# Setup on x and constants alone, state-space taps four to a bank, and two norms from one set of sums

## The chip, the cores and the metric

The kernel runs on one core of a Trainium2 chip, in one launch. The metric is the device time of the whole program in microseconds (us), lower is better. The engines: PE is TensorE (products and transposes; PEld are its weight loads), DVE is VectorE, ACT is ScalarE, POOL is GpSimd, and SP only issues DMAs. Each engine works through its own instructions in order and waits on semaphores for the others.

## What is computed

x has 512 positions of 1024 features (S = 512, D = 1024). Two blocks of layers follow one another:

```python
def first_block(x):
    for i in range(4):
        h = rms_norm(x, mix_norm_g[i])
        x = x + mixer(h)
        x = x + swiglu(rms_norm(x, ffn_norm_g[i]), ffn_w_gate_up[i], ffn_w_down[i])
    return rms_norm(x, final_norm_g)

def second_block(x):
    for l in range(2):
        h = rmsnorm(x, norm1_w[l]) * (1.0 + sc1) + sh1
        x = x + g1 * hybrid_mixer(h)
        h = rmsnorm(x, norm2_w[l]) * (1.0 + sc2) + sh2
        x = x + g2 * swiglu_2(h)
```

The mixers of the first block are fox attention, the S5 layer, a pooling and fox attention again; `hybrid_mixer` is a latent attention beside a state space layer. `rms_norm(x, g)` is x / sqrt(mean(x^2) + 1e-6) * g over the features. sc, sh and g1, g2 come from a small vector c and w_ada. The S5 layer is a linear state space of 64 groups with 16 channels and 64 complex states each. It is computed in chunks of eight positions: inside a chunk by a table of "taps" (the response of the layer at each distance, for the 16 x 16 channels of a group, with the skip gain d on the diagonal), between chunks by a scan of the states.

## The kernel before, in words

x lies transposed in the on-chip memory as `m.x`: 128 partitions by 8 blocks `k` of features by 512 positions. The program is a list of stages that `plan` sets up and `build` emits, each group of stages as one block: every engine has its own list of instructions, and all meet at the end of a block (the rows name L2900 or L2991 there). The two halves of a feed-forward net are one block; setup, FoxV, the S5 mixer, its GLU, the final norm and the second block's input projection are one block each. SP loads weights for the next chunks into two raw slots; a slot is free when DVE has made its low half.

Large products run as three single-pass products: weights and activations are split into a high part (ACT copies, `split_hi`, L1214) and a low part (DVE subtracts, `split_lo`, L1221). `Split.ahead(j)` prepares chunk j+1 while PE works on chunk j.

**Sums of squares.** `add_square` (L276 to L279) squares a block of x on DVE and adds it to `m.acc`. Whoever writes x calls it, `SplitDown` (L1573) in its second half for every block. `Stats` turns `acc` into 1/rms for every partition: PE sums the partitions against `mean_w` (L388), ACT takes the root (L402, after a `warm` activation at L400 that brings in the table), DVE inverts (L409) and builds four diagonal matrices (L411), PE spreads them to all partitions in bank 6 (L394). `keep_warm` (L284) issues filler matmuls. `SplitNorm` then makes h: DVE multiplies (L1185), ACT rounds to `h_hi` (L1172), DVE takes `h_lo` (L1180).

**Setup.** SP issues the constants, a table `spread` (64 x 1408 floats), x (2 MB), 18 rows of parameters, and four small loads for fox attention. PE (L2106) waits for x, for all 25 other loads and for the fills, then transposes x by blocks into four banks (L2114), and the parameters (L2117). DVE waits for the 25 loads, casts three constants, and per block copies it (L2136) and calls `add_square`; the columns come last (L2140). ACT makes `cact` and copies `spread` (L2123, L2124).

**FoxV** is the next block: ACT rounds the gate weights (L1638), DVE takes their rest (L1663), then `Stats`, then the first weight split between the diagonals and the use of bank 6, then h and the products (L1623 on).

**S5Mix.** POOL makes `v0` (eight groups q of powers of lambda times C, L941 to L947). DVE makes block-diagonal B matrices (`block(q)`, L966) in two buffers, input weights (`weights(q)`, L975 to L980), the rotation tables `ec` and `es` (`turns`, `table(n)`, L997 to L1017), and moves finished taps out (`keep(q)`, L989 and L990). PE does the input projection in four chunks f of weights (L812); `taps(q)` (L789), eight pairs of 32-row products into bank 4; `turn_w(q)` transposes the weights (L798). Behind each chunk stand taps: (0, 1), (2, 3), (4), (5, 6), then `turn_w(f)` for f < 3. `taps(q)` waits for `keep(q-1)`, since all use the same 128 columns of bank 4. Then come eight groups of transposed inputs (L824), gathered half by ACT and half by DVE (L927), `taps(7)`, and the loop of `inputs` (L838), `outputs` (L850, L852), `turn_w(q+3)` and `turn_y` (L860), in which DVE scans (L1057 to L1079). The taps go through DRAM: SP stores each q with its padding of zeros (L759), waits, and reads it back shifted in eight loads (L767), q = 0 to 2 at once, the others when a buffer is free. DVE's order is written out by hand from L1019: `block` 0 and 1, `weights(0)`, `keep(0)`, `block(2)`, `keep(1)`, `block(3)`, `weights(1)`, `turns()`, `table` 1, 2, 4 and 8, `keep(2)`, `block(4)`, `keep(3)`, `block(5)`, `weights(2)`, `table(16)`, `keep(4)`, `block(6)`, `table(32)`, `keep(5)`, `block(7)`, `keep(6)`, the eight gathers, `keep(7)`, the scans.

**FinalNorm** (L2841) is a block of its own: `Stats`, then DVE writes the normed x in place (L442) and squares it again for the next norm, then makes the gains (1 + scale) * w of the second block (L2859). **SecondIn** splits `wdt` (L2347, L2389), runs `Stats` and `SplitNorm` with those gains, and multiplies; its products (L1259 to L1261, L2333) go to banks 0 to 4, and at chunk 2 it squares latents in banks 5 and 6. x itself is not needed again before the block's output projection adds to it.

## Time and profile before

| | us |
|---|---|
| median of 3 runs | 4105.17 |
| the runs | 4106.72, 4099.12, 4105.17 |
| the profiled execution | 4099.89 |
| its span, from first to last instruction | 4098.1 |

| engine | busy us | share of the span |
|---|---|---|
| PE | 3765.1 | 92% |
| DVE | 2086.4 | 51% |
| ACT | 1073.3 | 26% |
| POOL | 1070.4 | 26% |

The mean granted clock of PE is 0.952 of full speed. Times in rows are us from the start of the span. A row of a timeline is one instruction or several alike that follow each other; "idle before" is how long the engine stood before it, and the arrow names what ended that. Rows of PE can overlap, since matmuls are pipelined.

### The profile page before, as it was taken

What the parts mean: (1) busy time and instruction counts of PE and PEld (TensorE: products, weight loads), DVE (VectorE), ACT (ScalarE), POOL (GpSimd) and SP (SyncE); (2) the same over time, 40 slices, a digit from 0 to 9 for tenths busy, and PEclk for the clock granted to TensorE, in tenths of its full rate; (3) what the DMA queues carried; (4) which work ended last, traced back from release to release, by engine and by line L of the source; (5) the groups of instructions that cost most, each with busy time, mean ns of one, the idle gap of its engine ahead of it and who ended that gap; (6) DMA issues with size and microseconds to landing.
All of it is one profiled execution on the core that took longest, in us unless ns stands there. A gap on an engine that the chain in (4) does not pass through costs nothing. (4 is left out here: it accounts for less than half of the span.)

```text
span 4098.1 us, 44475 instructions
## 1 busy us (share of the span) xinstructions
PE 3765.1 (92%) x16846; PEld 2898.0 (71%) x16846; DVE 2086.4 (51%) x2654; ACT 1073.3 (26%) x1473; POOL 1070.4 (26%) x835
## 2 busy tenths in 40 slices
PE   6889999778999979999898999897899999879999
PEld 5656888556788858887666888673578877347887
DVE  4445555775554575454445545565443345545334
ACT  2442222013221212222443222232321223332221
POOL 0342634610263416350342635001300000130000
PEclk9999999878999989999999999997899999889999
DMA  3114444211444324443112544210123322003332
GB/s 102 44 31 109 126 129 116 68 44 43 112 127 134 113 71 139 123 126 90 50 33 67 142 121 124 66 54 21 31 82 97 99 77 65 21 23 87 90 103 77
DMA packets 553376, 346.08 MB, mean 84 GB/s; under 512 B 32327, under 2 KB 534477, under 8 KB 553229
## 3 DMA queue, kind: packets, MB, share of 16 engines
q1 hardware_dynamic: 539404, 293.79, 25.5%
q0 software_dynamic: 13824, 50.34, 4.2%
q8 instruction: 91, 1.49, 0.2%
q14 instruction: 57, 0.46, 0.0%
HBM read 341.01 MB, written 3.08 MB: 84 GB/s over the span
## 5 line engine op out<-in xcount | busy, mean ns | idle before, releaser
L1259 PE MATMUL ps<-h_hi,w_hi 128*128 128x512 f32 x2880 | 1141.7, 396 | 33.0 <-DVE h_lo L2031 10.1
L1260 PE MATMUL ps<-h_lo,w_hi 128*128 128x512 f32 x2880 | 1126.1, 391 | 0.0
L1261 PE MATMUL ps<-h_hi,w_lo 128*128 128x512 f32 x2880 | 1125.7, 391 | 0.0
L1221 DVE TENSOR_TENSOR w_lo<-w,w_hi 128x2048 fp32r<-128x2048 f32 (+2 forms) x294 | 663.7, 2258 | 168.8 <-ACT w_hi L1214 166.3
L1214 ACT ACTIVATE w_hi<-w 128x2048 fp32r<-128x2048 f32 (+2 forms) x294 | 507.2, 1726 | 701.8 <-PE ps L1261 635.7
L1259 PEld LDWEIGHTS ps<-h_hi,w_hi 128*128 128x128 f32 x2880 | 544.2, 189 | 151.7 <-issue 35.4
L1261 PEld LDWEIGHTS ps<-h_hi,w_lo 128*128 128x128 f32 x2880 | 543.3, 189 | 115.2
L1260 PEld LDWEIGHTS ps<-h_lo,w_hi 128*128 128x128 f32 x2880 | 544.0, 189 | 108.4 <-issue 0.5
L1350 DVE TENSOR_TENSOR sg<-sg,ps 128x512 f32<-128x512 f32 x132 | 90.8, 688 | 719.4 <-ACT sg L1335 719.4
L1259 PE MATMUL ps<-a_hi,w_hi 128*128 128x512 f32 x1056 | 412.1, 390 | 0.0
L1261 PE MATMUL ps<-a_hi,w_lo 128*128 128x512 f32 x1056 | 411.0, 389 | 0.0
L1260 PE MATMUL ps<-a_lo,w_hi 128*128 128x512 f32 x1056 | 410.8, 389 | 0.0
L1335 ACT ACTIVATE sg<-ps 128x512 f32<-128x512 f32 x132 | 79.0, 598 | 1088.6 <-PE ps L1261 1088.5
L1132 POOL TENSOR_TENSOR w<-w,cact 128x1024 f32<-128x1024 f32 x96 | 184.5, 1922 | 452.3 <-PE ps L1318 452.0
L1134 POOL TENSOR_TENSOR w<-w 128x512 f32<-128x512 f32 x192 | 241.6, 1258 | 15.1
L1261 PEld LDWEIGHTS ps<-a_hi,w_lo 128*128 128x128 f32 x1056 | 198.2, 188 | 41.4
L1259 PEld LDWEIGHTS ps<-a_hi,w_hi 128*128 128x128 f32 x1056 | 198.2, 188 | 41.1 <-DVE w_lo L1221 0.3
L1260 PEld LDWEIGHTS ps<-a_lo,w_hi 128*128 128x128 f32 x1056 | 198.2, 188 | 41.0
L1123 POOL DMA_DIRECT2D w<-in_w_ada x96 | 88.7, 923 | 484.5 <-POOLq L2900 416.8
L1135 POOL TENSOR_TENSOR w<-w 128x128 f32<-128x128 f32 x96 | 195.1, 2032 | 7.5
L1879 POOL TENSOR_SCALAR misc<-misc,small 128x128 f32<-128x128 f32 (+3 forms) x128 | 138.1, 1086 | 204.2 <-DVE small L1896 203.9
L1911 DVE TENSOR_REDUCE small<-ps 128x1 f32<-128x128 f32 x192 | 93.2, 486 | 185.5 <-PE ps L1747 120.9
(445 smaller groups left out, 4137.9 us busy)
## 6 DMA issues: line engine op xcount, KB each, us to landing
w<-in_ffn_w_gate_up SPq DMA_DIRECT2D x176, 512.0 KB
w<-in_w_ada POOLq DMA_DIRECT2D x96, 512.0 KB, 6.9
w<-in_ffn_w_down SPq DMA_DIRECT2D x64, 704.0 KB
w<-in_w_gate_up SPq DMA_DIRECT2D x88, 512.0 KB
w<-in_w_down SPq DMA_DIRECT2D x32, 704.0 KB
w<-in_fox_w_in SPq DMA_DIRECT2D x32, 512.0 KB
w<-in_w_in SPq DMA_DIRECT2D x14, 1024.0 KB
w<-in_fox_w_in SPq DMA_DIRECT2D x8, 1024.0 KB
```

What stands on the lines that cost most here:

```text
L1123: nc.gpsimd.dma_start(three(m.ada_w[:, u % 2, :]), self.source(u)).then_inc(m.sem["ada_in"], 16)
L1132: m.pool(e, tt(three(p), three(m.ada_w[:, u % 2, :]), c, ALU.mult))
L1134: m.pool(e, tt(p[:, 0:n], p[:, 0:n], p[:, n:2 * n], ALU.add))
L1135: tt(p[:, 0:P], p[:, 0:P], p[:, P:2 * P], ALU.add).then_inc(m.sem["ada_summed"], 1)
L1214: last = nc.scalar.activation(hi, raw, ACT.Copy)
L1221: last = nc.vector.tensor_tensor(lo, raw, hi.bitcast(F32), ALU.subtract)
L1259: nc.tensor.matmul(out, hi, a[0][:, k, :], start=k == 0, stop=False)
L1260: nc.tensor.matmul(out, hi, a[1][:, k, :], start=False, stop=False)
L1261: return nc.tensor.matmul(out, lo, a[0][:, k, :], start=False, stop=k == kt - 1)
L1350: m.dve(e, nc.vector.tensor_tensor(t, m.sg[:, par(j), 0, :], m.ps[:, par(j) * 2 + 1, :], ALU.mult))
L1879: nc.gpsimd.tensor_scalar(self.pb[s % 2][t], self.pb[s % 2][t], self.stat(self.ri, s, t), None, ALU.mult).then_inc(m.sem["p_scaled"], 1)
L1911: nc.vector.tensor_reduce(self.stat(self.nm, s, t), m.ps[:, 2 + t % 2, 0:(t + 1) * P], AX.X, ALU.max, negate=True).then_inc(m.sem["max_rea ...
```

## The change

**Setup.** The constants have a semaphore of their own, and PE's transposes of x wait for them and for x alone; the parameters' transposes wait for the other 23 loads behind them. DVE only copies x. The sums of squares of the first norm are made by ACT from x as it was loaded (positions on partitions, four squares of 128 x 1024 with an accumulated output) and end as the root in `m.rms`; the first `Stats` is `known` and begins with the reciprocal. `spread` is loaded by the GLU's `sync`, as its last small load, and copied by ACT behind the GLU's third sigmoid. DVE squares the final gains into `final2`.

**S5.** `taps(0)` to `taps(3)` write four parts of bank 4, `taps(4)` to `taps(7)` four parts of bank 7; there are three `block` buffers, and two `keep`s. The zeros of the padding are stored once for all q.

**Final norm.** The stage is gone. The last down projection also sums squares of x times the final gains (`acc2`, in `m.std`). With r = 1/rms(x) and M = mean((x g)^2), the mean square of the normed x is r^2 M; `TwoStats` spreads r / sqrt(r^2 M + eps) in bank 6 for h, and r in bank 5, by which DVE scales x in place with the final gains after h is made. The next norm's gains take in the final gains.

```diff
@@ add_square
-    def add_square(self, e, k):
+    def add_square(self, e, k, final=False):
...
+        if final:
+            g = self.final2[:, k:k + 1]
+            if k == 0:
+                self.dve(e, self.nc.vector.tensor_scalar(self.acc2[:], self.acc[:], g, None, ALU.mult))
+            else:
+                self.dve(e, self.nc.vector.scalar_tensor_tensor(self.acc2[:], self.square[:], g, self.acc2[:], ALU.mult, ALU.add))
@@ S5Mix.sync_after
-        def store(q):
-            e.wait_ge(m.sem["k_ready"], m.at("k_ready", q + 1))
-            e.dma_start(self.scratch[q], self.k[q % 3]).then_inc(m.sem["k_stored"], 16)
-            e.wait_ge(m.sem["k_stored"], m.at("k_stored", 16 * (q + 1)))
+        rows = self.scratch.rearrange("q p n -> p q n")
+        e.wait_ge(m.sem["pads_clear"], m.at("pads_clear", 1))
+        e.dma_start(rows[:, :, 0:112], self.pad.rearrange("p (q n) -> p q n", q=1).broadcast_to([P, DK, 112])).then_inc(m.sem["k_stored"], 16)
+
+        def store(half):
+            e.wait_ge(m.sem["k_ready"], m.at("k_ready", half + 1))
+            e.dma_start(rows[:, 4 * half:4 * half + 4, 112:240], self.k[:, 4 * half:4 * half + 4, :]).then_inc(m.sem["k_stored"], 16)
+            e.wait_ge(m.sem["k_stored"], m.at("k_stored", 16 * (half + 2)))
...
+        store(0)
         for q in range(3):
-            store(q)
             load(q)
-        for q in range(3, DK):
-            store(q)
+        store(1)
         rest(e)
@@ S5Mix.tensor
-            for q in ((0, 1), (2, 3), (4,), (5, 6))[f]:
-                taps(q)
-            if f < 3:
-                turn_w(f)
+            if f == 2:
+                taps(0)
+                taps(1)
+                taps(2)
+            else:
+                turn_w(min(f, 2))
+        taps(3)
...
-        taps(7)
+        for q in range(4, DK):
+            taps(q)
@@ S5Mix.scalar
-            if f < 3:
-                weights(f)
+            if f != 2:
+                weights(min(f, 2))
@@ S5Mix.vector
         def block(q):
-            if q >= 2:
-                e.wait_ge(m.sem["tap_done"], m.at("tap_done", q - 1))
+            if q >= 3:
+                e.wait_ge(m.sem["tap_done"], m.at("tap_done", q - 2))
...
+        def keep(half):
+            e.wait_ge(m.sem["tap_done"], m.at("tap_done", 4 * half + 4))
+            src = ps[:, 4 + 3 * half, :].rearrange("p (q n) -> p q n", q=4)
+            nc.vector.tensor_copy(self.k[:, 4 * half:4 * half + 4, 16:P], src[:, :, 16:P])
+            for q in range(4):
+                last = stt(self.k[:, 4 * half + q, 0:16], m.c("eye16"), m.col("s5_d", 4 * half + q), src[:, q, 0:16], ALU.mult, ALU.add)
+            last.then_inc(m.sem["k_ready"], 1)
...
         weights(0)
+        for q in range(3):
+            block(q)
         weights(1)
         turns()
         for n in (1, 2, 4, 8):
             table(n)
         weights(2)
         table(16)
+        block(3)
+        block(4)
+        block(5)
+        keep(0)
+        table(32)
         block(6)
...
-        keep(7)
+        block(7)
+        keep(1)
@@ Setup.tensor
+        e.wait_ge(m.sem["consts_loaded"], 16)
         e.wait_ge(self.loaded.sem, 16)
-        e.wait_ge(self.par.sem, 16 * 25)
-        e.wait_ge(m.sem["filled"], 5)
...
+        e.wait_ge(self.par.sem, 16 * 23)
         for a in range(3):
@@ Setup.scalar
+        e.wait_ge(m.sem["filled"], 5)
+        e.wait_ge(self.loaded.sem, 16)
+        for t in range(ST):
+            m.acts(e, nc.scalar.activation(out[:, t % 2, :], xt[:, t, :], ACT.Square, accum_out=m.rms[:, t:t + 1]))
+        m.acts(e, nc.scalar.activation(m.rms[:], m.rms[:], ACT.Sqrt, bias=m.eps[:, 0:1], scale=1.0 / D))
         e.wait_ge(m.sem["turn_taken"], m.at("turn_taken", DK + 1))
-        m.acts(e, nc.scalar.activation(m.cact[:], m.cols[:, COL["c"]:COL["c"] + DK], ACT.Silu))
-        nc.scalar.activation(m.spread[:], m.tile(24, 3)[0:64].rearrange("p a s -> p (a s)")[:, 0:SPREAD.shape[1]], ACT.Copy)
+        nc.scalar.activation(m.cact[:], m.cols[:, COL["c"]:COL["c"] + DK], ACT.Silu)
@@ Setup.vector
             nc.vector.tensor_copy(m.x[:, k, :], m.ps[:, k % 4, :]).then_inc(taken.sem, 1)
-            e.wait_ge(taken.sem, taken.at(k + 1))
-            m.add_square(e, k)
@@ SecondIn.tensor, at chunk 2
+                if self.l == 0:
+                    e.wait_ge(m.sem["x_scaled"], m.at("x_scaled", 1))
@@ SecondIn.vector, behind ahead(0)
+        if self.l == 0:
+            e.wait_ge(m.sem["rms_spread"], m.at("rms_spread", 2))
+            for k in range(DK):
+                last = stt(m.x[:, k, :], m.x[:, k, :], m.col("final", k), m.ps[:, 5, :], ALU.mult, ALU.mult)
+            last.then_inc(m.sem["x_scaled"], 1)
+            e.wait_ge(m.sem["x_scaled"], m.at("x_scaled", 1))
@@ class TwoStats, in place of FinalNorm
+    def tensor(self, e):
+        for i, acc in enumerate((m.acc2, m.acc)):
+            for t in range(ST):
+                n = ST * i + t
+                last = nc.tensor.matmul(m.ps[:, 7, n:n + 1], acc[:, t * P:(t + 1) * P], m.mean_w[:, 0:1], start=n == 0, stop=True, skip_group_check=True)
+        last.then_inc(m.sem["sums_done"], 1)
+        m.keep_warm(6, 8)
+        for i in range(2):
+            for t in range(ST):
+                e.wait_ge(m.sem["diag_ready"], m.at("diag_ready", ST * i + t + 1))
+                last = nc.tensor.matmul(m.ps[:, 6 - i, t * P:(t + 1) * P], m.ones[:], m.diag[:, t, :], start=True, stop=True)
+            last.then_inc(m.sem["rms_spread"], 1)
+        m.keep_warm(7, 12)
...
+    def vector(self, e, between=None):
...
+        do(tt(first, first, m.cols[:, COL["final"]:COL["final"] + DK], ALU.mult))
+        e.wait_ge(m.sem["std_ready"], m.at("std_ready", 1))
+        do(nc.vector.reciprocal(r, r))
+        do(tt(b[:, 12:16], r, r, ALU.mult))
+        tt(b[:, 4:8], b[:, 12:16], m.ps[:, 7, 0:ST], ALU.mult).then_inc(m.sem["mean_ready"], 1)
+        e.wait_ge(m.sem["std_ready"], m.at("std_ready", 2))
+        do(nc.vector.reciprocal(b[:, 8:12], b[:, 8:12]))
+        do(tt(b[:, 8:12], b[:, 8:12], r, ALU.mult))
+        for t in range(ST):
+            nc.vector.tensor_scalar(m.diag[:, t, :], m.c("ident"), b[:, 8 + t:9 + t], None, ALU.mult).then_inc(m.sem["diag_ready"], 1)
+        e.wait_ge(m.sem["rms_spread"], m.at("rms_spread", 1))
+        for t in range(ST):
+            nc.vector.tensor_scalar(m.diag[:, t, :], m.c("ident"), r[:, t:t + 1], None, ALU.mult).then_inc(m.sem["diag_ready"], 1)
```

`keep_warm(6, 12)` at the end of the down projection stays.

## Rows read from the trace of the kernel before

**Rows 1.** The profile page: busy time, share and instructions of an engine.

```profile
PE 3765.1 (92%) x16846; PEld 2898.0 (71%) x16846; DVE 2086.4 (51%) x2654; ACT 1073.3 (26%) x1473; POOL 1070.4 (26%) x835
```

**Rows 2.** Waits, 0 to 75 us: us in all, times, longest.

```profile
PE ps L2114 <- DMA small<-in_fox_b_f: 16.0, 1, 16.0
```

**Rows 3.** DMA issues, 0 to 75 us: KB each, us to landing.

```profile
act<-in_x SPq DMA_DIRECT2D x1, 2048.0 KB, 10.6
```

**Rows 4.** Timeline, 0 to 75 us: start, duration, engine, line, operation.

```profile
17.07 0.69 DVE L2136 COPY xT<-ps 128x512 f32<-128x512 f32 x1 [0.50 <-PE ps L2114]
...
36.24 1.06 ACT L1638 ACTIVATE wfs<-wf 128x1024 fp32r<-128x1024 f32 x1 [0.27 <-PEq L2900]
...
37.32 1.28 ACT L400 ACT_TABLE_LOAD   x1
...
38.61 0.20 ACT L400 ACTIVATE warm<-eps 128x1 f32<-128x1 f32 x1
...
39.55 2.08 PE L394 MATMUL ps<-diag,ones 128*128 128x128 f32 x8
...
41.42 4.14 PE L284 MATMUL ps<-pastb,identb 128*128 128x512 bf16 x15
...
43.01 1.40 DVE L1185 SCALAR_TENSOR_TENSOR sg<-xT,cols,ps 128x512 f32<-128x512 f32 x2
...
45.28 0.51 PE L1623 MATMUL ps<-w_hi,h_hi 128*128 128x512 f32 x1
```

**Rows 5.** Waits of the S5 layer, 770 to 965 us.

```profile
PE ps L789 <- DVE arena L990: 38.2, 3, 36.8
...
DVE arena L989 <- PE ps L789: 16.4, 5, 6.9
...
DVE arena L975 <- PE ps L798: 1.0, 1, 1.0
```

**Rows 6.** Timeline of DVE in the S5 layer.

```profile
769.73 3.57 DVE L966 TENSOR_TENSOR sg<-rope,consts 128x128 f32<-128x128 f32 x4
...
835.07 0.27 DVE L989 COPY arena<-ps 128x112 f32<-128x112 f32 x1
...
872.43 1.73 DVE L927 COPY arena<-ps 64x256 f32<-64x256 f32 x4 [0.55 <-PE ps L824]
...
881.71 0.42 DVE L1060 TENSOR_TENSOR arena<-ps,arena 128x256 f32<-128x256 f32 x1 [0.52 <-PE ps L838]
```

**Rows 7.** Timeline around the final norm.

```profile
2602.99 0.69 DVE L1573 SCALAR_TENSOR_TENSOR xT<-ps,xT 128x512 f32<-128x512 f32 x1 [3.68 <-PE ps L1261]
...
2613.33 1.02 PE L388 MATMUL ps<-mean_w,acc 128*128 128x1 f32 x8 [0.30 <-PEq L2900]
...
2632.87 0.39 DVE L2859 SCALAR_TENSOR_TENSOR gains<-mod,cols 128x8 f32<-128x8 f32 x4
...
2642.48 0.58 PE L1259 MATMUL ps<-h_hi,w_hi 128*128 128x512 f32 x1
...
2661.22 2.29 DVE L1221 TENSOR_TENSOR w_lo<-w,w_hi 128x2048 fp32r<-128x2048 f32 x1 [6.58 <-ACT w_hi L1214]
```

**Rows 8.** Stretches of PE: length, busy (instructions), granted clock, DMA share, GB/s.

```profile
25.50:26.00 0.50, 0.00 (x0) 0.84 0.00 0
...
42.50:43.00 0.50, 0.50 (x2) 0.59 0.00 0
```

**Rows 9.** Timeline of PE and POOL in the S5 layer.

```profile
833.13 1.70 POOL L947 TENSOR_SCALAR arena<-arena 128x576 f32<-128x576 f32 x1
...
855.45 13.98 PE L812 MATMUL ps<-w,hT 128*128 128x256 f32 x64
...
871.33 1.94 PE L824 MATMUL ps<-consts,arena 128*64 128x128 f32 x16
...
900.86 1.97 PE L798 MATMUL ps<-consts,arena 128*128 128x128 f32 x8
```

**Rows 10.** DMA issues of the whole span.

```profile
arena<-s_taps SPq DMA_DIRECT2D x64, 64.0 KB, 2.4
```

More of the change, by code:

```diff
@@ L932, in gpsimd @@
         tt = nc.gpsimd.tensor_tensor
[L933 removed]
+        nc.gpsimd.memset(self.pad, 0.0).then_inc(m.sem["pads_clear"], 1)
         tmp = self.vtmp
@@ L2927, in build, with swiglu @@
             m.resume(ends)
-def swiglu(m, out, gate_up, down, norm, gate=None, units=None, side=None):
+def swiglu(m, out, gate_up, down, norm, gate=None, units=None, side=None, final=False):
     parts = []
```

151 lines of the change are left out of this document (75 added, 76 removed).

## The prediction

> **What bounds the kernel now.** The page first: TensorE (PE) is busy for 92% of the span [rows 1], so other engines' work counts only where PE stands still for it. The waits and timelines of the three stages that the diff touches show three such places.
>
> Setup: PE's first transpose waits 16.0 us for the last of 25 parameter loads [rows 2], although x (issued at 1.82 us) needs 10.6 us to land [rows 3]: 12.4 us. Then DVE copies x out of PSUM and sums its squares, 24 operations of 0.69 that start 0.73 apart from 17.07 us on, to the end of the columns' copy at 34.3; ACT copies the spread table behind that, and the next stage starts at 36.24, and its first real product at 45.28 [rows 4].
>
> S5 layer: PE stands 36.8 of 38.2 us for DVE's L990, the `keep` of a tap group [rows 5]: `taps(3)` can't overwrite bank 4 before `keep(2)`, which is queued behind the rotation tables. Later PE is the one awaited: DVE idles 16.4 + 1.0 us for taps and turned weights [rows 5], because the 14 us chunks still run. DVE works from 769.73 to its first gather at 872.43, and the first scan reads its input at 881.71 [rows 6].
>
> Final norm: the sums begin at 2613.33, the gains are done at 2633.26, and the first product of the next stage starts at 2642.48 [rows 7]. PE has only filler there.
>
> **Setup and the first norm.** Removed: 15 square and sum operations of DVE, the tail's spread copy on ACT, one DMA ahead of x. The spread table is 64 x 1408 x 4 B = 352 KB; against x's 2048 KB in 10.6 us less start-up I price it at 0.9 us (bounds 0 and 10.6 x 352/2048 = 1.8; the middle, since x shares the engines with it). So x lands at X = 11.5 us. The first copy starts 1.12 us after the transposes (15.95 to 17.07, [rows 2, 4]), eight copies follow at 0.73 and one of 0.56; early transposes need 0.23 each, which costs about 0.4 us of waiting. Columns are done at X + 7.9, `final2` and Silu at X + 8.1, and the stage border takes 0.25: the next stage starts at 19.9 instead of 36.24, -16.3. The other 23 loads need no new cover: they land by about 15.9 - 0.6, before the column transposes at X + 6.
>
> The cover of this is ACT: four squares of 128 x 1024, nearest row 1.06 each [rows 4] (bounds 1.06 and 1.3 with the accumulator), a Sqrt of 0.25, and at most two table loads of 1.28 [rows 4]: done by X + 7.3, just before DVE. I cost it at 0. If ACT is late, the border is.
>
> In the row, the first activation starts at 38.61, 0.01 us after the table load's end [rows 4]. The Trainium skill, "ScalarE: Activation LUTs", What ACT_TABLE_LOAD costs, gives 1.28 us and a drain of 1.38 behind it. By the rows the sum stands at 4058; by the page ACT would end at X + 10.1 and the sum would be 4060, an estimate from that page.
>
> In the next stage the sums and the Sqrt with its table load (1.28) fall away. Its DVE waits for the high part of the split (ACT's 1.06 us of L1638, then w_hi). The norm's vector work, which started 6.77 us into the stage at 43.01, starts about 5.8 in. But PE has now been idle for 4 us before the `diag` products at B + 2.9 (B is the stage's start). What the clock did in this place: granted 1.00 (2.4 GHz) it fell to 0.50 (1.2 GHz) within the half microsecond from 25.5, soon after the last transposes of setup, and rose in that from 42.5, 6.6 us after PE resumed with the stage [rows 8]. If PE is at the low level, the eight products take 2.08 [rows 4] to B + 5.0, then of the 15 filler matmuls those before B + 9.3 take 0.43 and the rest 0.21 (the row's 15 took 4.14, some 1.4 us of it at the low level, so 3 at 0.43 and 12 at 0.22): first product at B + 10.6, where it was B + 9.04. +1.5 (bounds -0.9, clock kept, and +3.0, all filler at 0.43).
>
> **S5.** `taps` move behind the chunks, four to a bank, and two `keep`s of 448 columns replace eight of 112. PE no longer meets the tables: chunks 0 to 3 run at 14 us each and end near 828 instead of 869.4 [rows 9]. Then `turn_w(2)` waits about 9 us for DVE's `weights(2)`, and `taps(3)` for `block(3)`. DVE is the path. Its 102.7 us [rows 6] hold 16.4 + 1.0 + 0.55 = 18.0 of waiting [rows 5, 6], which go. Seven keeps at 0.33 go (a copy of 0.27, [rows 6], and a small sum mostly beside it; 2.3 in all), block 7 moves behind (0.5), and one keep of 448 columns comes: no row has it; bounds 0.33 and 4 x 0.33 = 1.3; I take 1.1, as it has four sums and four times the columns under one start. New waits: 0.4 for the first turned weights, 0.3 for `taps(3)`, and 1.0 because `weights(2)` starts at 832 while POOL works to 834.8 [rows 9], and DVE's like work beside it runs slower. First gather: 872.4 - 18.0 - 1.7 + 1.7 = 854.4.
>
> The gathers took 7.9 us with 16 transposes (two q) in 1.94 [rows 9], at full clock. Now PE has idled, and eight transposes at the low clock take 1.97 (the turned weights at 900.86, [rows 9]). The last six q: 6 us at 1.9 each, then 0.97: end at 865.2, about 3 later than at the old pace. Behind them `block(7)` waits for `taps(4)`, `taps(7)` for it, and the second keep for that: 3.2 us to the scan's read, formerly 1.36. The read comes at 868.4 against 881.71: -13.3 (bounds -17, full clock, and -9, low clock throughout).
>
> SP gets the pad store (early, hidden), then one store of four q and three groups of loads: 845 + 2.7 + 3.7 + 2.4 [rows 10] = 854 for the first group, needed near 874. The second store delays the GLU's weights by nothing that is used before 964. The extra spread DMA (0.6 us of SP) and its ACT copy (1.38) lie beside eleven-microsecond chunks of the GLU: 0.
>
> **Final norm.** Eight more DVE operations in the last down projection: seven lie in idle gaps of 3.7 us [rows 7], the last adds 0.7, so the stage starts at B = 2614.0. Sixteen sum products (2.04 at twice [rows 7]) and DVE's 1.23 us split run side by side; ACT's Sqrt is ready at B + 2.7. Reciprocal, square, product, second Sqrt, reciprocal, product: six steps of about 0.2 to 0.25, so B + 4.4; four `diag` 0.9; spread to B + 6.0; second `diag` 0.9; `w_lo` 2.3 to B + 9.3; the first h chunk needs 2.5. First product at B + 11.8 = 2625.8 against 2642.48: -16.6 (bounds -18, -14). The eight in-place scalings of x cost 5.6 us (L1185's form, two in 1.40, [rows 4]) in a gap of 6.58 before L1221 at 2661.22 [rows 7]: 0, and at most 5.6 if that gap went. Behind the scalings waits the split of chunk 2.
>
> **Sum.** -16.3 + 1.5 - 13.3 - 16.6 = -44.7. The profiled execution took 4099.9 us (span 4098.1, so 1.8 around it, which stays): 4055.2. It lies 5.3 under the median of the three runs, 4105.2, and all four average 4102.7; I state 4102.7 - 44.7 = 4058.
>
> **Rivals.** (1) *The clock stays up* where PE's new idle stretches are broken: 2.4 + 3.0 less, 4052. For: setup's gap is broken by the column transposes, S5's by `turn_w(2)`. Against: after setup's transposes it fell at once [rows 8], and these gaps are of 4 us and more. 0.13.
> (2) *The low clock lasts* through the gathers and taps, since transposes with waits may not lift it: 4.2 more, 4062. For: at 900.86 the turned weights take 1.97, though small products of the states stand just ahead of them [rows 9]. 0.17.
> (3) *ACT ends setup*: a table load placed behind the wait for the columns adds 1.3, with slower accumulation 2: 4060. The Trainium skill's drain, named above, has this effect. 0.08.
> (4) *The change doesn't do what it says in part*: x is held up by the small loads and lands at 15.3, when the parameters do (-12.5 for setup), or the S5 stage loses half its gain in the circle of DVE and PE (`weights(2)`, `turn_w(2)`, `taps(3)`, `keep(0)`): 4062 to 4066. 0.09.
> (5) *Slower*: all taps of three groups now hang on one store, behind the pad store of 1024 pieces of 448 B. It decides once the first group lands over 20 us after its 854; to undo the other gains and add 8 us it must be 73 us late, 4111 and up. A landing in 2.4 us speaks against it [rows 10]. 0.02. The Trainium skill, "DMA: Bandwidth & Descriptors", Specifications, has transfers under 512 B turn into read-modify-write; no row here has this store.
>
> **How the numbers follow.** The forecast has 0.51, own range 4053 to 4063. With (1) to (3) and most of (4) the range is 4049 to 4067, ends moved out by some 3 us, since runs of one kernel lie 7.6 us apart. What a measurement can tell from no change is 0.2%, 8.2 us. Only (5) is slower: 0.02; 0.01 for within; 0.97 faster.
>
> **What would show it.** Setup: PE's first transpose near 11.5, next stage near 20, first product there 10.6 in, with 0.50 granted before it. S5: no PE wait over 12 us, DVE's first gather near 854 minus setup's 14.8, a 9 us PE wait for the turned weights. Final: one stage border fewer, first product 16 to 17 us sooner, no new wait at L1221. Wrong would be: the border of setup set by ACT, a PE wait for tap loads, or a DVE idle over 1 us between tables and gathers.

## The result and the profile after

The changed kernel takes 4066.26 us (median of four runs, 4062.85 to 4067.59) where the kernel before takes 4105.47 beside it (4099.12 to 4106.72). The medians lie 39 us apart; the ratio of the comparison is 0.9915 with a 95% interval of 0.9899 to 0.9931, a gain of 28 to 41 us. A second comparison gives 4061.86 against 4104.13, ratio 0.9899 (0.9877 to 0.9920), 33 to 50 us. The forecast was 4058, and the sum of its terms 44.7. The direction is as forecast; the gain is 5.5 us short of the sum in the first comparison and 2.4 in the second. The profiled execution took 4062.85 us, span 4061.1.

The engines' line of the page after the change; PE is as busy as it was (4 us more of 3765) [rows 1], DVE has 17 us less work:

```profile
PE 3769.1 (93%) x16819; PEld 2901.1 (71%) x16819; DVE 2069.4 (51%) x2631; ACT 1079.2 (27%) x1480; POOL 1070.7 (26%) x835
```

The timeline of the changed kernel, setup and the first norm (start, duration, engine, line, operation), which answers to [rows 2 to 4]:

```profile
9.55 1.28 ACT L2138 ACT_TABLE_LOAD   x1 [9.55 <-DMA act<-in_x]
9.62 5.62 PE L2124 MATMUL ps<-consts,act 128*128 128x128 f32 x32 [9.62 <-DMA act<-in_x]
...
10.85 1.06 ACT L2138 ACTIVATE sg<-act 128x1024 f32<-128x1024 f32 x1
...
15.56 1.28 ACT L2139 ACT_TABLE_LOAD   x1
16.36 0.55 DVE L2155 COPY cols<-ps 128x384 f32<-128x384 f32 x1
16.86 0.30 ACT L2139 ACTIVATE rms<-rms,eps 128x4 f32<-128x4 f32 x1
16.94 0.17 DVE L2158 TENSOR_TENSOR final<-cols 128x8 f32<-128x8 f32 x1
17.17 1.28 ACT L2141 ACT_TABLE_LOAD   x1
18.47 0.21 ACT L2141 ACTIVATE cact<-cols 128x8 f32<-128x8 f32 x1
...
21.72 2.08 PE L404 MATMUL ps<-diag,ones 128*128 128x128 f32 x8 [6.16 <-DVE diag L423]
...
23.59 5.21 PE L293 MATMUL ps<-pastb,identb 128*128 128x512 bf16 x15
...
28.45 0.58 PE L1635 MATMUL ps<-w_hi,h_hi 128*128 128x512 f32 x1
```

Read it from the top. x lands at 9.6 us and PE starts on it at once, where it stood until 16.0. DVE is done at 17.1, ACT only at 18.7: three table loads of 1.28 us stand on its way, the first of them behind the wait for x. The next stage begins at 18.94 (36.24 before), and its first product comes at 28.45, 16.8 us sooner than in [rows 4]. The eight `diag` products take 2.08 us and 15 fillers 5.21: the low clock, as forecast.

Waits of the S5 layer in the changed kernel (745 to 853 us), which answer to [rows 5]:

```profile
PE ps L815 <- DVE arena L1001: 11.8, 1, 11.8
...
PE ps L806 <- DVE sg L987: 4.0, 2, 3.8
```

and its DVE timeline, which answers to [rows 6]:

```profile
839.51 1.72 DVE L948 COPY arena<-ps 64x256 f32<-64x256 f32 x4
842.42 0.85 DVE L948 COPY arena<-ps 64x256 f32<-64x256 f32 x2 [1.19 <-PE ps L844]
...
851.60 0.62 DVE L1006 COPY arena<-ps 128x448 f32<-128x448 f32 x1 [0.89 <-PE ps L806]
...
852.90 0.42 DVE L1072 TENSOR_TENSOR arena<-ps,arena 128x256 f32<-128x256 f32 x1
```

PE's 36.8 us for `keep` are gone; in their place PE waits 11.8 for `weights(2)` and 3.8 for `block(3)`. DVE has no pause before the gathers, so DVE is the path, and the scan reads its input at 852.90 instead of 881.71: 28.8 us sooner, of which 15.4 were won before the stage.

Last, the timeline at the norm between the halves, which answers to [rows 7]:

```profile
2590.48 0.75 DVE L288 SCALAR_TENSOR_TENSOR std<-square,final,std 128x512 f32<-128x512 f32 x1
2591.75 1.06 ACT L2371 ACTIVATE wds<-wdt 128x1024 fp32r<-128x1024 f32 x1 [17.09 <-PEq L2968]
2591.77 1.02 PE L2882 MATMUL ps<-mean_w,std 128*128 128x1 f32 x8 [0.96 <-PEq L2968]
2592.65 1.03 PE L2882 MATMUL ps<-mean_w,acc 128*128 128x1 f32 x8
...
2595.95 0.88 DVE L2923 TENSOR_SCALAR diag<-consts,both 128x128 f32<-128x128 f32 x4
...
2603.45 0.47 PE L1271 MATMUL ps<-h_hi,w_hi 128*128 128x512 f32 x1 [1.33 <-DVE h_lo L1192]
```

From the first sum to the first product it takes 11.7 us (2591.77 to 2603.45), where it took 29.2.

**Where the lead comes and goes.** The table below matches each DVE instruction of a trace with the same one in the first trace of before, and gives the difference of the two starts at chosen times of before (negative is a lead). All kernels of the study stand in it; their edits follow. Differences given in the text are taken before rounding, so they can be 0.1 off the table's. 762 is the start of the S5 layer, 882 its first scan, 1034 the third gate of the GLU behind it, 1900 to 2206 the fox attention of layer 3, 2604 and 2646 the two sides of the norm between the halves, 3404 to 3702 the state space and attention of the second half's second layer.

| trace | 165 | 762 | 882 | 1000 | 1034 | 1900 | 2206 | 2604 | 2646 | 3404 | 3702 |
|---|---|---|---|---|---|---|---|---|---|---|---|
| before, second | 1.1 | -2.0 | -2.1 | -2.1 | -2.2 | -2.5 | -2.3 | -2.9 | -2.9 | -0.9 | 3.5 |
| before, third | 0.1 | 0.5 | 0.3 | 0.5 | 0.4 | 0.2 | 0.1 | -0.7 | -0.7 | 0.1 | 0.1 |
| changed | -12.9 | -15.4 | -28.8 | -30.1 | -24.6 | -24.8 | -21.1 | -22.2 | -38.9 | -41.6 | -37.2 |
| changed, again | -17.8 | -21.3 | -35.8 | -34.4 | -29.4 | -29.0 | -26.7 | -27.1 | -43.8 | -39.9 | -34.7 |
| load twice | -17.6 | -17.8 | -32.3 | -30.5 | -22.9 | -22.6 | -21.0 | -22.6 | -39.9 | -39.7 | -31.1 |
| load late | -12.8 | -18.0 | -31.7 | -28.9 | -28.4 | -28.6 | -25.5 | -26.6 | -43.8 | -44.8 | -40.4 |
| combined | -18.0 | -20.8 | -34.3 | -31.2 | -30.9 | -31.1 | -28.1 | -28.9 | -45.2 | -45.4 | -34.5 |
| tables early | -18.9 | -22.5 | -37.0 | -35.2 | -34.9 | -35.1 | -28.8 | -29.4 | -45.8 | -48.2 | -43.8 |
| setup alone | -17.2 | -16.8 | -17.0 | -16.6 | -15.7 | -16.2 | -12.3 | -13.3 | -12.8 | -22.8 | -18.2 |
| taps alone | 2.0 | 0.2 | -13.5 | -10.9 | -11.1 | -11.5 | -6.2 | -6.8 | -6.8 | -6.1 | -1.8 |
| norm alone | -0.6 | -3.7 | -4.2 | -9.6 | -9.0 | -9.2 | -7.8 | -8.4 | -24.8 | -23.7 | -19.4 |
| half v0 | -15.7 | -15.9 | -46.4 | -51.6 | -50.8 | -50.9 | -45.5 | -46.4 | -63.1 | -62.7 | -58.1 |
| delay short | 9.5 | 8.9 | 8.9 | 9.3 | 9.3 | 9.1 | 12.4 | 12.5 | 12.8 | 10.2 | 14.6 |
| delay long | 17.0 | 16.2 | 14.7 | 16.7 | 16.7 | 16.2 | 17.2 | 16.8 | 17.1 | 17.7 | 22.3 |

The first trace of the change shows three losses behind its first columns. Between 1000 and 1034 us the lead falls by 5.6 us, in the stage into which the spread load was moved. Between 1900 and 2206 it falls by 3.7, and between 3404 and 3702 by 4.4, in code that the change doesn't touch. A fourth lies ahead of the first column: at 70 us the lead is 16.8, at 165 it is 12.9, in the first layer's gates and attention, which are untouched too (the second trace keeps its 17.7). Untouched code also gains: 5.5 us between 882 and 1000 with the norm alone, and 10.0 between 2646 and 3404 with setup alone. The experiments ask after both kinds.

### The profile page after: what moved, and what is told of

Same layout as the page of the kernel before. It is cut to its first block and busy times, and to the rows that moved or that the text cites. A ratio compares the mean times of both kernels' runs of the same rounds, so it can differ in the third digit from the quotient of the medians.

```text
span 4061.1 us, 44371 instructions
## 1 busy us (share of the span) xinstructions
PE 3769.1 (93%) x16819; PEld 2901.1 (71%) x16819; DVE 2069.4 (51%) x2631; ACT 1079.2 (27%) x1480; POOL 1070.7 (26%) x835
## 5 line engine op out<-in xcount | busy, mean ns | idle before, releaser
L1271 PE MATMUL ps<-h_hi,w_hi 128*128 128x512 f32 x2880 | 1142.0, 397 | 36.4 <-DVE h_lo L1192 12.3
```

The lines of the kernel that those rows point to most:

```text
L1271: nc.tensor.matmul(out, hi, a[0][:, k, :], start=k == 0, stop=False)
```

## Experiments

**The changed kernel again.** No edit.

> The changed kernel once more, so that later kernels have it beside them on the same chip, and for a second trace of it. If the places where its lead over the kernel before shrinks are caused by its code, they are the same in this trace: the lead falls by 4 to 5 us between the first gate of the layer with the spread matrix's load and the third (ScalarE waits about 9.4 us for w<-in_s_w_glu, then PE 3.5 us), by 3 to 4 us in the fox attention of layer 3, and by 5 to 6 us in the state space of the second half's second layer. If the clock's phases do it by chance, the last two move or vanish while the first stays. Time 4062 to 4068, that is 0.9895 to 0.991 of the kernel before.

Measured: 4061.86 us against 4104.13. ScalarE again waits 10.2 us for the GLU's weights, and the lead falls by 5.1 us there (1000 to 1034), by 2.3 and 5.3 in the two later places. All three come back. The time is just under the 4062 to 4068 that I expected. But the lead at 762 is 21.3 us where it was 15.4, with the same code: two executions of one kernel differ by 6 us at a place in the middle, so a single pair of traces gives a stage's gain well and the total badly.

**The spread load behind the weights.** In the GLU's stage of the changed kernel:

```diff
-        e.dma_start(m.tile(24, 3)[0:64]..., d["spread"]).then_inc(m.sem["spread_loaded"], 16)
+    def sync_after(self, e, rest):
+        rest(e)
+        e.dma_start(m.tile(24, 3)[0:64]..., d["spread"]).then_inc(m.sem["spread_loaded"], 16)
...
-            if j == 2:
+            if j == 6:
                 e.wait_ge(m.sem["spread_loaded"], m.at("spread_loaded", 16))
```

> The changed kernel with one load moved: the 352 KB of the spread matrix are issued behind the stage's stream of weights instead of ahead of it, and copied at the seventh gate, not the third. Theory (the load ahead of the stream makes the stream late): the wait of ScalarE for w<-in_s_w_glu goes back from 9.4 us to about 5.7, the one of PE for the low halves (3.5 us) vanishes, the lead at the third gate stays at 28 to 29 us instead of 24.6, and the run ends 3 to 5 us ahead of the changed kernel: 4058 to 4063. Rival (the stream is late for another reason, such as the stage starting earlier against its loads, and the low clock of 995 to 1000 us comes by itself): the waits and the time stay within 1 us of the changed kernel's.

**The load issued twice.** The changed kernel with a second copy of the same 352 KB into unused tiles, behind the first and ahead of the weights; the copy on ACT waits for both.

> The changed kernel with the spread matrix's load issued twice ahead of the weight stream (the second copy into unused space), everything else the same. Theory (each 352 KB ahead of the stream makes it late by its own transfer time): ScalarE's wait for w<-in_s_w_glu in this stage goes from 10.2 us to 13 to 15, and the lead over before falls between the first and the third gate by 8 to 10 us, not 4 to 5: some 4 us slower than the changed kernel. Rival (only the queue's order or ScalarE's copy at the third gate costs, not the bytes): waits and lead within 1 us of the changed kernel's.

The group of the w_hi splits on ACT around the GLU (busy and mean ns of one, then idle before them and what ended it). Before:

```profile
L1214 ACT ACTIVATE w_hi<-w 128x2048 fp32r<-128x2048 f32 x7 | 13.4, 1908 | 6.8 <-DMA w<-in_s_w_glu 5.7 <-PEq L2900 1.1
```

changed:

```profile
L1226 ACT ACTIVATE w_hi<-w 128x2048 fp32r<-128x2048 f32 x7 | 13.4, 1910 | 11.5 <-DMA w<-in_s_w_glu 10.2 <-PEq L2968 1.4
```

load late:

```profile
L1226 ACT ACTIVATE w_hi<-w 128x2048 fp32r<-128x2048 f32 x7 | 13.4, 1910 | 7.8 <-DMA w<-in_s_w_glu 6.4 <-PEq L2972 1.4
```

load twice:

```profile
L1226 ACT ACTIVATE w_hi<-w 128x2048 fp32r<-128x2048 f32 x7 | 13.4, 1908 | 13.8 <-DMA w<-in_s_w_glu 12.4 <-PEq L2969 1.4
```

ACT's wait for the weights is 5.7 us before, 10.2 with the load ahead of the stream, 12.4 with two, and 6.4 with the load behind it. What PE pays is in its own waits of the stage. Changed:

```profile
PE ps L2236 <- DVE w_lo L1233: 3.5, 1, 3.5
```

load twice:

```profile
PE ps L2237 <- DVE w_lo L1233: 5.7, 1, 5.7
```

and with the load late it is 0.6. The copy of the table on ACT was moved together with the load, but it isn't what holds PE up: in the changed kernel it starts at 1008.97, and PE's pause ends at 995.57. The pause has a price behind it as well. The stretch of PE after the pause (length, busy time and instructions of PE, PEld, DVE, ACT and POOL, granted clock, DMA share, GB/s) in the changed kernel:

```profile
995.57:1001.00 5.43, 5.43 (x17) 4.27 (x18) 4.91 (x5) 0.70 (x1) 0.00 (x0) 0.69 0.72 193
```

and with the load late:

```profile
993.60:999.00 5.40, 5.40 (x25) 4.42 (x24) 4.93 (x5) 1.64 (x1) 0.00 (x0) 1.00 0.71 194
```

After 3.5 us without work PE runs at a granted clock of 0.69 and gets through 17 products where it gets through 25 at 1.00. The second trace of the changed kernel shows the same (0.64 behind a pause of 3.6), and no trace with the load late does.

In the table the step from 1000 to 1034 is +5.6 and +5.1 for the changed kernel, +7.7 with two loads, +0.5 with the load late. The run with the late load takes 4058.30 (ratio 0.9892, 0.9871 to 0.9914), 3.6 under the changed kernel on the same chip; two loads take 4068.15 (0.9905, 0.9878 to 0.9931). The intervals overlap, so it is the waits and the table that show the cause, with no load, one and two ahead of the stream: the bytes ahead of a stream that ACT already waited for are paid by PE, as a pause and as the low clock behind it. The medians of one chip agree: two loads 4068.15 (4065.23 to 4071.19), the load late and the tables early (below) 4056.54 (4056.04 to 4057.13), 11.6 us apart, of which 1.2 are the tables'. The second load cost less than I expected (2.2 us of ACT's wait more, not 3 to 5, and a step of 7.7 us, not 8 to 10).

**The three parts alone**, each put into the kernel before (the setup part with its spread load late).

> The kernel before with the first part alone (setup waits for x and the constants, squares on ScalarE, first norm from known sums), its spread load behind the weight stream as in the run above. By the traces of the changed kernel the first product of the first norm comes 16.8 us sooner and the norm's end 15 to 16: 4089 to 4091, a gain of 14 to 17 us. Rival (the gain is partly given back by the clock in the following attention, or by loads that come no sooner than before): a gain under 13 us, and the lead falls below 15 before the first gated product ends.

> The kernel before with the second part alone (taps four to a bank, stored twice). Theory: the stage gains the 13.4 us that the changed kernel gained in it whatever comes before it, so 4091 to 4093; PE waits 11 to 12 us for the third weights and 3 to 4 for the fourth block. Rival (half of it is the place of the clock's low stretches in this stage, which an earlier setup had shifted): a gain under 10 us or over 16, with the granted clock of the eight ut groups other than in the changed kernel (L844 3.57 us each).

> The kernel before with the third part alone (the last norm of the first half and the norm behind it from one set of sums). In the three traces of kernels with this part the lead grows by 16.7, 16.7 and 17.3 us between the last square of the down product and the first low half behind it. Theory: the same here, 16 to 18 us locally, and 4086 to 4090 for the run. Rival (the added squares, x's scaling or the lower clock behind the shorter stage give some back): the local gain is the same but the run gains under 13 us.

| part | local gain in its trace | gain of medians | ratio (95%) |
|---|---|---|---|
| setup | 17.2 (at 165) | 17.0 | 0.9967 (0.9952 to 0.9982) |
| taps | 13.7 (762 to 882) | 9.8 | 0.9973 (0.9959 to 0.9988) |
| norm | 16.4 (2604 to 2646) | 11.6 | 0.9970 (0.9958 to 0.9982) |

The local gains are those of the changed kernel: 13.4 and 14.6 for the taps, 16.7 and 16.7 for the norm. Their sum is 47.3. The medians sum to 38.4, but each carries several microseconds of scatter (the kernel before alone spreads over 26 us in its 23 runs here, standard deviation 7), and the kernel with all three parts and the late load gains 45.8. So the parts add up, within what these runs can tell. I had expected the taps to be worth 13 in the run (4091 to 4093); it came to 4094.31, and the norm (4086 to 4090 expected) to 4092.62. Those gains, 9.8 and 11.6, lie under the marks of 10 and 13 that I had set for the rivals (for the taps, that the place of the low clock makes part of the gain; for the norm, that some of it is given back). Their intervals reach from 5 to 17 and from 7 to 17 us, so the medians can't decide it; in the traces the local gains are whole, and the rest is what untouched code does.

**The kernel before, twice more.** No edit. This is for the losses in untouched code.

> The kernel before, unchanged, for a second trace of it. All four traces of kernels with parts of the change lose their lead in the same two untouched places against the first trace of before: 2 to 5 us in the fox attention of layer 3 (from 1900 to 2205 us of before) and 4 to 6 us in the state space of the second half's second layer (3400 to 3700). Theory (the clock's low stretches fall by chance, and the first trace of before was lucky there): this trace loses too, so that its place at 3700 us is 4 to 8 us behind the first trace's, and its time is near the 4104 of the last comparison rather than 4100. Rival (something of the change, such as the shifted start, makes the later stages slower): this trace stays within 1 us of the first in both places.

> The kernel before, unchanged, a third trace. The second trace lost 4.5 us against the first between 3403 and 3702 us, as all changed kernels do, but nothing between 1900 and 2205, where they lose 1.4 to 5.3. Theory (chance, both): this one moves by a few us in either place, and its time is near 4104. Rival (in the fox attention of layer 3 the loss belongs to the shifted start): again within 0.5 us of the first trace from 1900 to 2205.

The second trace did lose 4.5 us between 3404 and 3702, the third nothing; neither lost more than 0.2 between 1900 and 2206. That is half of what I expected of the second, and by the sign that I had set, the third spoke for the rival, in which the loss in the fox attention belongs to the shifted start. The first and third traces lie within 0.7 us of each other in every column, so they count as one, and a trace of before can be 4.5 us luckier than another in one place. By runs, the unchanged kernel came to 4099.87 and 4104.07 against 4104.17 and 4104.56 beside it; the first pair gives a ratio of 0.9985 with an interval of 0.9972 to 0.9998 for a kernel against itself. So an interval that just misses 1 says nothing here.

**Nothing but a delay.** The kernel before with work for nobody at the end of setup:

```diff
+        for i in range(8):      # 16 in the long one
+            m.acts(e, nc.scalar.activation(out[:, i % 2, :], xt[:, i % 4, :], ACT.Copy))
```

> The kernel before with eight copies of a 128x1024 tile into unused space at the end of setup on ScalarE (about 1.2 us each, so 9 to 10 us), nothing else. Theory (a shift alone moves the low clock to places where it costs): the delay of 9 to 10 us at the first norm has grown by 1 to 6 us through the fox attention of layer 3 (1900 to 2205 us), where granted clock of 0.66 shows near 1960 us of before as in the changed kernels, and by another 4.4 through 3403 to 3702; the run is 11 to 20 us slower than before. Rival (the changed code does it): the delay stays within 1 us of its first value through both, with the granted clock of the first trace, and the run is 9 to 10 us slower.

> The same with sixteen copies, 19 to 20 us. By the theory the clock's pattern is another again, so the growth differs from the short delay's by some us in either direction and may be none in one place; by the rival the run is 19 to 20 us slower with no growth. Where the two delays differ by other than the 9 to 10 us of their copies, that difference is what a shift alone can do to this kernel's time.

The stretches of the fox attention of layer 3 (1900 to 2206 of before) and of the second state space (3480 to 3541), from the same first instruction to the same last one in each trace: length, busy time and instructions of PE, PEld, DVE, ACT and POOL, granted clock, DMA share, GB/s. Before, first trace:

```profile
1900.50:2205.50 305.00, 267.71 (x1200) 192.86 (x1201) 140.98 (x259) 121.32 (x233) 88.57 (x96) 0.94 0.18 52
3480.10:3541.00 60.90, 47.04 (x177) 26.44 (x178) 32.40 (x43) 20.02 (x50) 11.93 (x10) 0.84 0.00 1
```

before, second trace:

```profile
1898.03:2203.19 305.16, 267.89 (x1200) 193.10 (x1201) 141.00 (x259) 121.23 (x233) 88.40 (x96) 0.94 0.18 52
3479.12:3543.89 64.77, 50.92 (x178) 28.67 (x179) 31.47 (x43) 20.07 (x50) 12.08 (x10) 0.79 0.00 1
```

changed:

```profile
1875.72:2184.39 308.67, 272.12 (x1200) 194.85 (x1201) 140.94 (x259) 121.31 (x233) 88.55 (x96) 0.93 0.18 52
3438.41:3503.18 64.77, 50.91 (x178) 28.67 (x179) 31.47 (x43) 20.11 (x50) 12.09 (x10) 0.79 0.00 1
```

short delay:

```profile
1909.59:2217.95 308.36, 272.07 (x1200) 195.00 (x1201) 140.97 (x259) 121.23 (x233) 88.38 (x96) 0.93 0.18 52
3490.19:3554.96 64.77, 50.93 (x178) 28.67 (x179) 31.47 (x43) 20.07 (x50) 12.09 (x10) 0.79 0.00 1
```

long delay:

```profile
1916.73:2222.75 306.02, 269.06 (x1200) 192.79 (x1201) 141.00 (x259) 121.33 (x233) 88.60 (x96) 0.94 0.18 52
3497.79:3562.61 64.82, 50.97 (x178) 28.69 (x179) 32.55 (x43) 20.09 (x50) 11.82 (x10) 0.79 0.00 1
```

The instruction counts are the same but for one record, DVE, ACT and POOL do the same work, and PE is 4 us busier where the granted clock is 0.93 or 0.79 rather than 0.94 or 0.84. The state space has two lengths in these traces, 60.9 and 64.8 us, and which of them a trace gets can't be the change's doing, since the second trace of before and both delays get the long one. The fox attention takes 308.4 us behind the short delay, 308.7 in the changed kernel, 306.0 behind the long delay and 305 in the three traces of before. So a shift in time by itself moves PE's stretches of low clock and costs or saves 1 to 4 us in each of these places. The widest swing of the study is in another untouched place, the first state space of the second half (2755 to 2795 of before). The changed kernel, again:

```profile
2712.63:2756.59 43.96, 43.96 (x140) 24.45 (x140) 15.16 (x24) 13.84 (x41) 10.11 (x8) 0.66 0.00 1
```

setup alone:

```profile
2743.30:2773.22 29.92, 29.92 (x140) 16.73 (x139) 14.97 (x23) 13.86 (x41) 10.32 (x8) 1.00 0.00 1
```

The same 140 products take 44.0 us at a granted clock of 0.66 and 29.9 at 1.00; the three traces of before take 40.4 to 40.6, the changed kernel's first trace and both delays 37.0.

The Trainium skill, "TensorE: Matmul & The Clock Gate", Part 1, describes the gate's own timing as running free of the kernel; that fits these traces.

The runs: 4118.15 and 4122.22 against 4107.24, that is 10.9 us for a delay of 10.2 (ratio 1.0021, 1.0009 to 1.0033) and 15.0 for one of 17.7 (1.0042, 1.0026 to 1.0058). For the short one I had expected 11 to 20. The rest (+4.4 and +4.6 at the end of the traces) isn't there in the medians, which would fit if the phases, that is the places where the low clock falls, even out over many runs; that is not shown. What remains open is why all ten traces in the table of kernels with a part of the change lose 1.4 to 6.4 us between 1900 and 2206 while the long delay loses only 1; the short delay's 3.4 shows that a shift can do it, and chance is not excluded with so few traces.

**Three further edits**, on the kernel with the late load:

```diff
+        nc.scalar.activation(m.warm[:], m.eps[:], ACT.Square)       # (a) ahead of the wait for x
         e.wait_ge(self.loaded.sem, 16)
...
+        nc.scalar.activation(m.warm[:], m.eps[:], ACT.Silu)         # (a) ahead of the wait for the columns
...
-        m.keep_warm(7, 15)
+        m.keep_warm(7, 10 if self.known else 15)                    # (b)
...
         turns()
+        weights(2)                                                  # (c)
         for n in (1, 2, 4, 8):
             table(n)
-        weights(2)
```

> The changed kernel with the late spread load and three edits where its trace showed time to be had. (a) Setup: a Square and a Silu of one column ahead of the waits, so that their table loads (1.28 us each) lie in idle time: the first norm's stage starts 1.1 to 1.4 us sooner (18.9 to about 17.7). (b) The first norm's filler 10 products long instead of 15: the first product another 1 to 1.7 us sooner, though if the products then wait for h behind DVE (1.26 us a tile) most of it is lost again by the end of the first chunk. (c) State space: the third weights, six operations of 512 columns, ahead of the small tables instead of behind them. If a DVE operation that meets GpSimd's costs about 1.1 to 1.3 us whatever its size (L1017 0.19 and 1.09), the six large ones lose little there and six small ones win 0.9 each behind GpSimd's end: the scan starts 2 to 3 us sooner, and PE's wait of 12 us for these weights goes. Rival: large operations pay the contention too (1.54 against 0.69), so nothing is won. Together 3 to 6 us ahead of the run with the late load alone: 4052 to 4056.

Measured 4056.02 (ratio 0.9879, 0.9861 to 0.9896), at the upper end of what I expected. (a) held: the next stage starts at 18.03 instead of 19.12 in the kernel it is built on. (c) won nothing: 762 to 882 gains 13.5 us against 13.7 with the late load alone, and the third weights took 1.15 to 1.89 us an operation for five of their six in the new place, where all six had taken 0.69 in the old one; PE's wait for them became a wait of 17.1 for `block(3)`. The rival was right, and its reason is in the last experiment. On (b) this kernel alone says nothing; the next one does.

**Only the tables**, edit (a) on the kernel with the late load.

> The changed kernel with the late spread load and of the three further edits only the first: a Square and a Silu of one column ahead of the waits of setup. The combined kernel's trace had the stage's start 1.1 us sooner, nothing in the state space (13.5 us against 13.7), and the run came out 2.3 us below the late load's by medians of different jobs. Theory: the other two edits were worth nothing, so this one is where the combined kernel is, 4055 to 4058, and the first norm's wfs starts at 18.0 us. Rival (the shorter filler was worth something that the clock hid): 4058 or more, and the first chunk of the first layer ends later than the combined kernel's.

ACT's timeline of this kernel at the end of setup:

```profile
9.69 1.06 ACT L2139 ACTIVATE sg<-act 128x1024 f32<-128x1024 f32 x1 [7.05 <-DMA act<-in_x]
...
16.01 1.28 ACT L2141 ACT_TABLE_LOAD   x1
17.30 0.20 ACT L2141 ACTIVATE warm<-eps 128x1 f32<-128x1 f32 x1
17.41 0.19 ACT L2143 ACTIVATE cact<-cols 128x8 f32<-128x8 f32 x1
17.87 1.06 ACT L1650 ACTIVATE wfs<-wf 128x1024 fp32r<-128x1024 f32 x1 [0.27 <-PEq L2974]
```

The first square starts as x lands, the Silu runs as soon as DVE is done, and the stage begins at 17.87 instead of 19.12: 1.2 us won for two one-column activations. 4056.54 us, four runs within 1.1 us, ratio 0.9877 (0.9852 to 0.9903). It is the combined kernel's time, so (b) and (c) together were worth nothing that shows. This is the simplest kernel that is ahead of both: 48 us under before, and 5 under the changed kernel in the second comparison, which ran on another chip.

**Half of GpSimd's work.** On the kernel with the late load, `v0` of the last four groups is filled with zeros instead of computed, so the taps of half the channel groups are left out of the result:

```diff
+            if q >= 4:
+                nc.gpsimd.memset(self.v0[q][0], 0.0)
+                nc.gpsimd.memset(self.v0[q][1], 0.0).then_inc(m.sem["v0_ready"], 1)
+                continue
             tt(vr, c[0], w[0], ALU.mult)
```

> The changed kernel with the late spread load, and GpSimd computes its part of the taps (seven operations of 576 columns a group) for the first four groups alone; the other four are filled with zeros, so the taps of half the channel groups are left out. It asks what DVE pays for GpSimd's work beside it: in this stage DVE operations of 32 to 256 columns take 1.1 to 1.3 us while GpSimd works and 0.19 to 0.43 when it is done. Theory (each DVE operation waits for the GpSimd operation that holds the way to memory): with GpSimd done about 38 us sooner some 30 operations lose 0.8 to 0.9 us each, DVE reaches the gathers 15 to 25 us sooner, and with PE's last chunk then the next limit (it ends at 808 us) the first gather comes 12 to 22 us sooner: the run 4038 to 4048. Rival (the long durations come from DVE's own operands, not from GpSimd): durations stay and the first gather moves by under 2 us.

DVE and POOL in the kernel with the late load:

```profile
788.28 1.20 POOL L962 TENSOR_TENSOR arena<-s_c,sq 128x576 f32<-128x576 f32 x1
788.48 1.04 DVE L1036 TENSOR_TENSOR small<-small 128x32 f32<-128x32 f32 x1
789.44 1.16 POOL L963 TENSOR_TENSOR sg<-s_c,sq 128x576 f32<-128x576 f32 x1
789.56 1.12 DVE L1027 TENSOR_TENSOR arena<-arena,small 128x64 f32<-128x64 f32 x1
790.56 1.16 POOL L964 TENSOR_TENSOR arena<-s_c,sq 128x576 f32<-128x576 f32 x1
790.71 1.09 DVE L1028 TENSOR_TENSOR arena<-arena,small 128x64 f32<-128x64 f32 x1
```

and with half of the work left out:

```profile
781.63 0.58 POOL L964 MEMSET arena<- 128x576 f32 x1
782.15 0.58 POOL L963 MEMSET arena<- 128x576 f32 x1
782.42 0.21 DVE L1031 TENSOR_TENSOR arena<-arena,small 128x32 f32<-128x32 f32 x1
```

In the upper rows each DVE operation, 32 or 64 columns, ends within 0.1 us of the end of the POOL operation beside it (789.52 and 789.48, 790.68 and 790.60, 791.80 and 791.72), whatever its own size. In the lower rows a 128x32 operation takes 0.21 beside POOL's memset, and from the start of the turns to the start of `weights(2)` DVE needs 18.5 us (775.27 to 793.79) instead of 42.7 (773.18 to 815.88). The Trainium skill, "SBUF — State Buffer", Who interferes with whom, has just this: a DVE instruction with two SBUF inputs and a GpSimd instruction that reads SBUF exclude each other, and one that only writes does not; this trace agrees on both counts, with 1.04 to 1.12 us for the one and 0.21 for the other. The run takes 4039.09 (ratio 0.9829, 0.9799 to 0.9859), 19 us less than with the late load; the scan's lead is 46.4 us instead of 31.7, where I expected 12 to 22 more, and got 16.8 more within the stage.

## Why the prediction was right or wrong

**Setup and the first norm, -14.8 forecast, -16.6 to -17.7 measured** (first product, in the six traces with this setup as it stands). X was 9.6, not 11.5. x is issued 0.6 us sooner and lands 8.3 us behind its issue instead of 10.6 [rows 3], so the spread load had cost it 2.3 us: more than the 0.9 that I took, and more than the bound of 1.8 by its share of the bytes. The cover by ACT, priced at 0, was not there: ACT ends 1.6 us behind DVE. That is rival (3), with three table loads rather than two, the first of them placed behind the wait for x. The two errors have opposite signs, and the stage starts at 18.94 for 19.9. The drain that the Trainium skill, "ScalarE: Activation LUTs", What ACT_TABLE_LOAD costs, gives did not show: the first square starts 0.02 us behind the table load's end (10.83 and 10.85). The norm's lengthening was forecast at 1.5 us and was 0.5 (9.5 from the stage's start to the first product, where it was 9.04): PE had stood 6.2 us before the `diag` products, not 4, and the clock was low as forecast, but it rose at 27.2 us, 8.3 into the stage, not 9.3, and the filler began 0.3 sooner. The forecast's own terms (fillers at 0.43 to B + 9.3, then at 0.21) add up to B + 10.35 and not 10.6, and its upper bound to +2.4 and not +3.0. With the same code the first product came 8.4 to 9.5 us into the stage in the six traces, so this term depends on where the clock rises and was not to be had to 1 us. (The forecast's 24 operations of 0.69 on DVE are 23, and the 24th is the columns' copy of 0.56; its sum doesn't use the count.)

**S5, -13.3 forecast, -13.4 to -14.6 measured** in the seven traces with this part (762 to 882). The wait of PE for `weights(2)` was forecast at 9 and is 11.8, which costs nothing since DVE is the path; a gather took 1.7 us while DVE waited for PE (842.42 to the next at 844.13), where 1.9 was forecast for the low clock. The term holds by its steps: within the stage the first gather comes 17.5 us sooner (18.0 forecast), and from there to the scan's read it takes 13.4 (14.0).

**The norm between the halves, -16.6 forecast, -16.3 to -17.3 measured** in the seven traces with this part (2604 to 2646). The first product comes 11.7 us behind the first sum (11.8 from the stage's start in the forecast), and nothing waits at the added scalings.

**The step that failed** is one sentence: "The extra spread DMA (0.6 us of SP) and its ACT copy (1.38) lie beside eleven-microsecond chunks of the GLU: 0." I priced the issue and the copy, not the bytes. The load stands ahead of the stage's weight stream in SP's queue, and that stream was already late for ACT: 5.7 us of wait in the kernel before, in a row that the forecast doesn't have. 352 KB more made it 10.2, and what ACT and DVE could no longer make up became 3.5 us of PE's, 2.9 more than with the load late, and a low clock behind them. It cost 4.6 to 5.1 us in the traces (5.1 and 5.6 between 1000 and 1034, less the 0.5 that goes there with the load late) and 3.6 in medians. The forecast looked at who waits behind the second store of the taps, and passed over it here.

**The sum, and the rivals.** I made the sum against one execution and set it against the mean of four, 4102.7. Traces of one kernel show one state space at two lengths 4 us apart (the one used for the forecast has the short one), and starts in mid-kernel 6 us apart, so a difference of 5 us between two single executions needs no cause in the change. Take the load's 5 us off 44.7, and add the 2.3 by which setup's term was too small: 42. The comparisons gave 39 and 42; with the load late it is 46, where 47 is due. Of the 8.3 us between the forecast of 4058 and the 4066.26 measured, 2.8 come from the base (4102.7 for 4105.47), 2.7 from the load less what setup gave more, and 2.8 are left. That the first comparison's interval ends at 41 is left to the scatter; nothing here shows a further cause. Of the rivals, the clock did not stay up (1). It did not stay low through all the gathers (2): they take 1.7 us a group from the third on, and the sixth and seventh 2.1 together (847.09 to 849.15). ACT did end setup (3). Of (4), x landed sooner, not later, and S5 kept its gain. No wait for a tap load appears (5).

## What to carry to other kernels

A transfer that is moved has to be priced by its bytes at its new place in the queue: look up who waits for the transfers behind it, and whether that wait is already there. Put a one-column activation ahead of the wait so that the table loads in idle time. And judge a stage's gain from the start times of the same instructions in two traces at the stage's two ends; the total of two single traces carries the clock's phases, here up to 14 us in one stretch of unchanged code.

## What the runs showed that was not expected

GpSimd's operations on 576 columns hold up DVE's in the S5 layer: 42.7 us instead of 18.5 for 57 operations of 32 to 256 columns. 27 of the 57 took 1.04 to 1.45 us, whether they have 32 columns or 256, and 25 slipped through at their short time of 0.09 to 0.43; with 512 columns it is 1.15 to 1.89 (0.69 alone). Reordering them won nothing. Half of GpSimd's work there is worth 19 us of the run, if it could be had elsewhere or earlier; that was not tried.

The length of a stretch of unchanged code depends on when it starts. One state space took 60.9 us in two traces, 64.8 to 65.1 in twelve and 72.2 in one (the combined kernel's); another took 29.9 to 44.0; a fox attention took 305 to 311. With nothing but a delay of 10.2 us ahead of it, the kernel showed the longer of the two usual lengths of the first, and a fox attention of 308.4.
